# One stream of weights over two transformer blocks, the first block's layers written out, and the last modulation rows sent ahead of weights

## The reference

```
for l in range(2):
    h = x @ w_in[l]                      # all four branches and their gates
    ...                                  # RWKV-7, latent attention, convolution, attention over mem
    proj = einsum('bsnc,ncd->bsnd', branches, w_o_branch[l])
    gates = sigmoid(merge.reshape(B, S, 4, D) + b_gate[l])
    out = sum(gates * proj, axis=2) @ w_out[l]
    x = layer_norm(DEEPNORM_ALPHA * x + out, ln_g[l], ln_b[l])
```

```
for i in range(2):
    mod = silu(c) @ w_ada[i] + b_ada[i]              # and the same with c_ctx
    hx = rms_norm(x, g_mix[i]) * (1 + sc1) + sh1
    x = x + ga1 * (concat(attention, pool_mix, fourier_mix)(hx @ w_in[i]) @ w_out[i])
    x = x + ga2 * swiglu(rms_norm(x, g_ffn[i]) * (1 + sc2) + sh2)
```

## Time and profile before

| what | us |
|---|---|
| median of three runs | 3662.97 (3659.33 to 3665.39) |
| the profiled execution | 3664.74 |
| its span, first to last instruction | 3662.9 |
| PE busy | 3265.1 (89%) |
| PE weight loads | 2559.1 (70%) |
| DVE busy | 1445.6 (39%) |
| ACT busy | 1167.1 (32%) |
| POOL busy | 1485.3 (41%) |

### The profile page before, as it was taken

One profiled execution on the slowest core, in us unless ns is written; L12 is line 12 of the kernel. 1 busy time (PEld: TensorE's weight loads), 2 busy tenths in 40 slices (PEclk: granted clock), 3 DMA queues, 4 the chain that ended last, 5 costly groups with the idle time before them and its releaser, 6 DMA issues. The chain is left out here.

```text
span 3662.9 us, 53263 instructions
## 1 busy us (share of the span) xinstructions
PE 3265.1 (89%) x21306; PEld 2559.1 (70%) x21306; DVE 1445.6 (39%) x2330; ACT 1167.1 (32%) x1880; POOL 1485.3 (41%) x831
## 2 busy tenths in 40 slices
PE   6789999999677899999996888989999978889998
PEld 5674676788456746767874655778888865568786
DVE  4642265777645322757776225320000021530000
ACT  5213333322242234334222425332112232532121
POOL 4411553444243215534442236533334423745453
PEclk9999999999888999999998899999999989999999
DMA  3001122455120011225551200111111111022222
GB/s 110 16 11 50 63 88 75 167 195 198 39 86 8 20 46 58 94 67 183 191 190 35 97 35 1 47 58 64 58 64 64 64 55 46 1 75 98 87 98 81
DMA packets 75035, 282.21 MB, mean 77 GB/s; under 512 B 8320, under 2 KB 8320, under 8 KB 73888
## 3 DMA queue, kind: packets, MB, share of 16 engines
q1 hardware_dynamic: 74784, 278.76, 22.1%
HBM read 276.62 MB, written 2.10 MB: 76 GB/s over the span
## 5 line engine op out<-in xcount | busy, mean ns | idle before, releaser
L130 POOL TENSOR_TENSOR lows<-ring,highs 128x1024 fp32r<-128x1024 f32 x376 | 919.5, 2446 | 1734.1 <-ACT highs L122 1734.1
L154 PE MATMUL ps<-x_high,highs 128*128 128x512 f32 x1936 | 773.9, 400 | 81.2 <-ACT highs L122 67.7
L157 PE MATMUL ps<-x_low,highs 128*128 128x512 f32 x1936 | 760.6, 393 | 0.0
L122 ACT ACTIVATE highs<-ring 128x1024 fp32r<-128x1024 f32 x376 | 397.2, 1057 | 797.4 <-PE ps L154 458.5
L154 PEld LDWEIGHTS ps<-x_high,highs 128*128 128x128 f32 x1936 | 367.8, 190 | 170.9 <-ACT highs L122 70.0
L157 PEld LDWEIGHTS ps<-x_low,highs 128*128 128x128 f32 x1936 | 367.7, 190 | 78.3 <-issue 3.5
L585 PE MATMUL ps<-x_high,lows 128*128 128x512 f32 x1072 | 264.7, 389 | 0.0
L2350 DVE TENSOR_TENSOR hidden_scratch<-ps,hidden_scratch 128x512 f32<-128x512 f32 x66 | 39.7, 603 | 552.8 <-PE ps L1747 545.3
L585 PEld LDWEIGHTS ps<-x_high,lows 128*128 128x128 f32 x1072 | 201.2, 188 | 41.8
L162 PE MATMUL ps<-hidden_parts,highs 128*128 128x512 f32 (+1 forms) x528 | 189.9, 360 | 12.0 <-PEq L2284 12.0
L166 PE MATMUL ps<-hidden_parts,lows 128*128 128x512 f32 (+1 forms) x528 | 190.0, 360 | 0.0
(11 more groups left out here) (400 smaller groups left out, 5957.0 us busy)
## 6 DMA issues: line engine op xcount, KB each, us to landing
ring<-in_w SPq DMA_DIRECT2D x402, 512.0 KB, 3.5
merging<-in_ada SPq DMA_DIRECT2D x48, 512.0 KB, 4.3
BR<-in_ada SPq DMA_DIRECT2D x48, 512.0 KB, 4.3
more_tiles<-in_dft SPq DMA_DIRECT2D x2, 2048.0 KB, 8.3
X<-in_xT SPq DMA_DIRECT2D x4, 512.0 KB, 7.5
X<-in_memT SPq DMA_DIRECT2D x2, 1024.0 KB, 5.0
merging<-in_cond SPq DMA_DIRECT2D x4, 512.0 KB, 4.7
out<-xT SPq DMA_DIRECT2D x1, 2048.0 KB, 6.3
```

The lines of the kernel that those rows point to most:

```text
L122: nc.scalar.activation(self.high(n), self.chunk(n), ACT.Copy).then_inc(self.hi_made, 1)
L130: nc.gpsimd.tensor_tensor(self.low(n), self.chunk(n), self.high(n).bitcast(F32), ALU.subtract).then_inc(self.lo_made, 1)
L154: mm = nc.tensor.matmul(ps, high, xhigh, start=start, stop=False)
L157: nc.tensor.matmul(ps, high, xlow, start=False, stop=False)
```

## The change

The body of the first block's loop is written out for both layers (a Python loop), with tile names that carry the layer. One `Stream` now numbers all chunks of both blocks through; each stage adds the base of its layer, `send`, `hi` and `lo` stop at the end of all chunks, and the first chunk of a layer is counted in `used` like every other. The clearing stages behind the layers are gone, both in the first block and in the second. The out stage of the first block sends two chunks further and splits one more, as the down stages of the second block do at a layer's end. In most stages SP sends the one chunk that its slot allows before it clears, and the `cond` vectors and the `dft` table are also issued before the clears. At the end of the merge stage the rows 40 to 47 are all sent ahead of chunk 45.

```
--- before.py
+++ after.py
@@ class Stream
     def send(self, sp, upto):
-        for n in range(self.sent, upto):
+        for n in range(self.sent, min(upto, NCHUNKS)):
             last = n - RING
-            if last in self.splits:
-                sp.wait_ge(self.lo_made, self.splits.index(last) + 1)
+            if last in self.place:
+                sp.wait_ge(self.lo_made, self.place[last] + 1)
...
@@ build
+        def weights(n):
+            if n < SECOND:
+                return A["w1"][n // NCHUNK1, n % NCHUNK1, :, :]
+            return A["w2"][(n - SECOND) // NCHUNK2, (n - SECOND) % NCHUNK2, :, :]
+
+        split = [NCHUNK1 * layer + n for layer in range(LAYERS) for n in SPLIT1] + list(range(SECOND, NCHUNKS))
+        stream = Stream(WR, weights, split)
...
@@ attention
-            clear(sp, other)
             if beside is not None:
                 beside.send(sp)
+            clear(sp, other)
...
@@ first
-    with nc.Fori(0, LAYERS) as layer:
-        stream = Stream(WR, lambda n: A["w1"][bass.ds(layer, 1), n, :, :].rearrange("l p c -> p (l c)"), SPLIT1)
+    for layer in range(LAYERS):
+        base = layer * NCHUNK1
...
@@ first, merge
-                clear(sp, other)
                 for c in range(2):
                     sp.dma_start(CB[:, c, :], A["cond"][c].partition_broadcast(P)).then_inc(S("cond"), 16)
+                stream.send(sp, n0 + RING)
+                clear(sp, other)
                 for t in range(48):
-                    stream.send(sp, n0 + min(t + RING + (0 if t < 2 else 3), 48 + RING - 1))
+                    stream.send(sp, n0 + min(t + RING + (0 if t < 2 else 3), 45))
                     if t >= 4:
                         sp.wait_ge(S("ada"), 2 * (t - 3))
...
+                stream.send(sp, n0 + 48 + RING - 1)
@@ first, out
+                stream.send(sp, n0 + RING)
                 clear(sp, other)
-                stream.send(sp, n0 + 8)
+                stream.send(sp, n0 + 8 + RING - 1)
...
-                for t in range(3, 9):
+                for t in range(3, 10):
                     stream.hi(nc, act, n0 + t)
...
-                stream.lo(nc, pool, n0 + 8)
+                stream.lo(nc, pool, n0 + 9)
@@ behind each pass of the first block, and behind each layer of the second
-        S, other = stage()
-        with nc.Block() as block:
-            @block.sync
-            def _(sp):
-                clear(sp, other)
-                clear(sp, WR[3])
-                clear(sp, WR[4:])
@@ second, Norm.tensor
-                if n_first:
+                if n_first is not None:
                     nc.tensor.matmul(PS[:, 3, 0:1], C("ones", P), C("ones"), start=True, stop=True).then_inc(used, 1)
@@ second, mixing
+                sp.dma_start(Z[:, 0:8 * T], A["dft"]).then_inc(S("dft"), 16)
                 clear(sp, other)
-                sp.dma_start(Z[:, 0:8 * T], A["dft"]).then_inc(S("dft"), 16)
                 sp.wait_ge(S("dft"), 16)
@@ second, project (and the same in up)
+                    stream.send(sp, first + RING)
                     clear(sp, other)
-                    stream.send(sp, min(first + chunks + RING - 1, NCHUNK2))
+                    stream.send(sp, first + chunks + RING - 1)
```

More of the change, by code:

```diff
@@ L114, in hi @@
     def hi(self, nc, act, upto):
-        for n in range(self.hi_at, upto):
-            if n in self.splits:
-                s = self.splits.index(n)
+        for n in range(self.hi_at, min(upto, NCHUNKS)):
+            if n in self.place:
+                s = self.place[n]
                 self.wait(act, n)
@@ L198, in build @@
         XH, XL = sb("x_high", [P, DK, T], F32R)[:, :, :], sb("x_low", [P, DK, T], F32R)[:, :, :]
+        def weights(n):
[4 more added lines that the diff above has]
+        stream = Stream(WR, weights, split)
         with ExitStack() as one:
-            first(nc, one, A, PS, XH, XL, WR, mods, stage, loaded)
+            first(nc, one, A, PS, XH, XL, stream, mods, stage, loaded)
         with ExitStack() as two:
-            second(nc, two, A, PS, XH, XL, WR, mods, stage, constants, stored)
+            second(nc, two, A, PS, XH, XL, stream, mods, stage, constants, stored)
 def clear(sp, sems):
@@ L469, in _, with first @@
                     finish(pairs[i - 2].group)
-def first(nc, ctx, A, PS, XH, XL, WR, mods, stage, loaded):
+def first(nc, ctx, A, PS, XH, XL, stream, mods, stage, loaded):
     def sb(name, shape, dt=F32):
@@ L1425, in first @@
         room.close()
-        n0 = FIRST["merge"]
+        n0 = base + FIRST["merge"]
         room = ExitStack()
-        BL, BH = (room.enter_context(nc.sbuf_tensor(f"branches_{part}", [P, NB * WT, T], F32R))[:, :, :] for part in ("low", "high"))
-        Y = room.enter_context(nc.sbuf_tensor("merging", [P, 18 * T], F32))
+        BL, BH = (room.enter_context(nc.sbuf_tensor(f"branches_{part}{layer}", [P, NB * WT, T], F32R))[:, :, :] for part in ("low", "high"))
+        Y = room.enter_context(nc.sbuf_tensor(f"merging{layer}", [P, 18 * T], F32))
         def YT(i, n=1):
@@ L1539, in first @@
         room.close()
[L1540 removed]
+        n0 = base + FIRST["out"]
         room = ExitStack()
[L1542 to L1544 removed]
+        MH, ML = (room.enter_context(nc.sbuf_tensor(f"merged_{part}{layer}", [P, DK, T], F32R))[:, :, :] for part in ("high", "low"))
+        RR, SQ = (room.enter_context(nc.sbuf_tensor(name, [P, DK, T], F32))[:, :, :] for name in (f"residuals{layer}", f"residual_squares{layer}"))
+        Y = room.enter_context(nc.sbuf_tensor(f"merged{layer}", [P, 16 * T], F32))
         RST, RUN = YT(0), YT(1)
@@ L1679, with second @@
 NCHUNK2 = _at
-def second(nc, ctx, A, PS, XH, XL, WR, mods, stage, constants, stored):
+SECOND = LAYERS * NCHUNK1
+NCHUNKS = SECOND + LAYERS * NCHUNK2
+def second(nc, ctx, A, PS, XH, XL, stream, mods, stage, constants, stored):
     def sb(name, shape, dt=F32):
@@ L1712, in second @@
         update = layer < LAYERS - 1
-        stream = Stream(WR, lambda n: A["w2"][layer, n, :, :], list(range(NCHUNK2)))
-        used = WR[4]
+        base = SECOND + layer * NCHUNK2
+        used = stream.used
         room = ExitStack()
@@ L1732, in mark @@
         def mark(n, first):
-            return used if n and first else None
+            return used if first else None
         def gemm(pe, n, outs, ready=None):
```

61 lines of the change are left out of this document (28 added, 33 removed).

## The result

The changed kernel takes 3631.31 us (median of 4 runs, 3628.04 to 3635.67); the kernel before, in the same comparison, 3661.34 (3659.33 to 3665.39). The ratio is 0.9911, with a 95% interval of 0.9897 to 0.9924: 33 us less, give or take 5, by the ratio, 30.0 by the medians. Forecast were 3634 us and a range of 3615 to 3648. The profiled execution took 3628.04 us, the fastest of its four; its span is 3626.2 where the one before had 3662.9, its mean granted clock 0.960 where that had 0.956.

The account below looks back on a forecast made before the run. PE was taken to bound the stages, leaving its idle stretches to win: 37.9 us won less 6.8 lost, 31.1 net, from the profiled 3664.7 to 3634 us, with an 8-in-10 range of 3615 to 3648.

Parts of the forecast that it names:

- A: First block, layer 0 to 1: PE's 12.3 us wait shrinks to a 0.5 us stage change, gain 11.8 us.
- rival 4: Written-out code fetched late, or loop's end costs little: A gives perhaps half of its 11.8, 3640 us; chance 0.08.
- B: First block to second: earlier start (3.7) and one high part less in ACT's chain (0.9), gain 4.6 us.
- D: End of the program: output goes 0.5 us behind DVE in place of 3.7, gain 3.2 us.
- F: The `dft` table, twice: its transfer goes 3.2 us earlier, cutting PE's 7.91 us wait, gain 6.4 us.
- C: Second block, layer 0 to 1: 17.3 us up to PE's first product become 10.2, gain 7.1 us (3.2 to 8.5).
- E: Start of the merge stage, twice: third chunk goes some 3 us earlier, ACT can use 2.4, gain 4.8 us.
- G: End of the merge stage, twice: chunk 45, queued behind row 47, comes late and PE restarts later, cost 6.8 us.
- Rivals 1 and 3: Merge stage's end: 1, chunk 45 not late, 3612 us, chance 0.12; 3, G grows past the gains, 3679 us, chance 0.04.
- rival 1: Merge stage's end: chunk 45 is not late, so G wins 14.6 us instead of losing 6.8, 3612 us; chance 0.12.
- Rival 2: E and F are hidden and C gives only the removed stage, 3649 us; chance 0.13.
- H: Other sends ahead of clears, and clears behind the last send in the attention stage: both worth nothing.

Follow-up runs that it names:

- loop_out: Kernel before with only the first block's two layers written out in place of the loop: 3663.31 us, ratio 0.9995 to the kernel before.
- stages_back: Changed kernel with an empty stage of 50 clears put back at the end of each of the four layers: 3647.02 us, ratio 0.9937.
- cap50: Changed kernel with the merge stage's old transfer order, chunk 45 no longer queued behind row 47: 3630.44 us, ratio 0.9898.
- cap48: Changed kernel with rows 43 to 47 sent ahead of chunks 48 and 49 only, so not ahead of chunk 45: 3631.2 us, ratio 0.9901.
- clears_first: Changed kernel with the 50 clears put back ahead of each stage's first transfers, wherever they had been moved: 3644.78 us, ratio 0.9933.
- pace28: Like pace30, with the merge's 48 rows' sums spread over the first 28 products in place of 30: 3613.4 us, ratio 0.9848.
- pace30: Changed kernel with the merge queue's chunk lead over rows falling by one every 8 rows, no cap at chunk 45: 3611.92 us, ratio 0.9850.

## Why the prediction was right, point by point

A (layer 0 to 1 of the first block), forecast 11.8, is 11.94, and its step is shown in three parts. I had named the loop's jump as part of it without a price; it is a third. The rule that I cited from the Trainium skill, Runtime: NRT & Kernel Launch, Instruction fetch mechanics, that a taken branch out of the window stalls, fits the turn: 3 us without an instruction behind the taken branch, next to none where the same branch isn't taken. That those 3 us are fetching isn't shown by itself. Written-out code doesn't come late to an extent that shows: from PE's first matmul of a layer to its last pass 971.7 and 969.8 us, before 969.3 and 971.4, and loop_out isn't slower than the kernel before, so rival 4 is out.

B (first block to second), 4.6, is 4.60, with some luck: its start gave 3.96 and not 3.7, its chain 0.64 and not 0.9. D (the end), 3.2, is 3.4. F (the tables), 6.4, is 6.9.

C (layer 0 to 1 of the second block), 7.1, is 8.2, close to its upper bound of 8.5. The term that was mis-sized is the 5.6 us up to ACT's free moment: it measured 4.6, because PE's sums no longer ran at the low clock level behind the clearing stage. The sum took them over from the earlier trace rows as they were, and stages_back brings their 2.05 us back. The low part's 2.3 us stood as forecast. The bound of 8.5 had another reason, DVE's normalising not being held; it wasn't held, but PE waits for `x_low`, which ends behind POOL's low part all the same, so that bound held by luck.

E (start of the merge stage), 4.8, is 3.6, the term furthest off. Its step "the chunk goes some 3 us earlier" held: SP issues it 0.8 us behind PE's start of the stage in place of 3.9. But from issue to use it took 7.4 us (648.52 to 655.93) where it took 5.8 before (652.91 to 658.71), so ACT still waits 0.96. Ahead of it in the queue stand the two vectors, in both kernels, and moving the chunk ahead of them takes ACT's wait away. What made the transfer longer isn't shown.

G (end of the merge stage), 6.8 lost, is 6.3 by the milestones of the changed kernel, 9.6 against cap50 and 5.9 in the kernel before. Row 43's second sum ended at 903.9 and not at 906.0, and chunk 45 was used at 908.86 and not at 911.3, because the whole stage stood about 2 us earlier, while the sum for G is made in the times of the kernel before. PE's stall came out near the forecast (8.59 for 8.9), since PE was earlier by as much. Rivals 1 and 3 are out. What I had read wrongly in the earlier trace rows is the late rows' cause. I took the waits of 1.93 and 2.28 us for the whole of what the old order costs, and from this came rival 1's 7.3 us a layer for a queue that sends rows in time at the end. cap48 does that and gains nothing over cap50. The rows are late throughout the stage, behind chunks that wait for the ring, and at the end POOL's holds take the place of each wait that is removed.

Rival 2 (E and F hidden) is out by clears_first, and it bears out the first half of H: the other sends show nothing.

The forecast of 3634 us stood on the profiled execution of the kernel before, 3664.74; by the medians 30.0 us were gained and by the ratio 33, with 31.1 forecast. The agreement of the sum owes something to errors that cancel: C gave 1.1 more than forecast, E 1.2 less.

## What to carry to other kernels

A queue on which a send waits for one consumer and the next send for another makes the second consumer run at the first one's pace: here giving the rows more lead over their use was worth some 10 us of two merge stages, read against the old order at their end, and undoing the new order there about as much again. The new order at the end moved most of a stall from one place to another, and lost a few us by it. When a wait of an engine is taken away, look for what was hidden by it, in this kernel the 2.4 us instructions of POOL beside which DVE's take 2 us longer. And where a stage boundary is on the path, split it by one experiment each for the loop, the clears and the cold pipeline: here they were 4.0, 3.1 and 4.5 us, of which the loop alone, in the timing, would have passed for nothing. The clears are one instruction a semaphore, 50 of them in 2.8 us (649.0 to 651.8 in the changed kernel); clearing several at once, or none in some stages, wasn't tried.

## What the runs showed of the hardware that I had not expected

- Two-input instructions of DVE that begin beside a subtraction of POOL end behind it, by 1.1 us for a sum in both rows above, so the delay depends on the phase: 1.2 us sums took 2.0 when POOL's instruction had begun 1.5 us before, 3.4 when 0.1 before. Over a stage this averages out to a mean of 1.5 us a sum in the changed kernel and 1.9 to 2.0 in pace28, where DVE hardly pauses (15 us of 228).
- The end of a hardware loop's pass cost 4.0 us on the path, the exit 0.5, measured by writing the same two passes out; 3 us of the 4.0 pass between SP's taken branch and its next instruction.
- Fifty semaphore clears with their stage cost 3.1 us at two boundaries, 3.5 at the end and 4.5 where the parameters' transfer and ACT's normalising stand behind them. The last is 1.4 longer because PE's idle time ahead of its sums grows to 4.86 us and they run at the low clock level.
- The same four sums of PE, from layer 0 to 1 of the second block, ran at a granted clock of 0.87 behind 1.77 us of idle PE and at 0.50, the 1.2 GHz level, behind 4.86 and 5.20 us.
- The recurrence, the same in all kernels, ran with more stretches at the low clock level in one execution than in another: 3.1 us of difference between the traces of before and after in layer 1, 3.7 between those of pace30 and pace28 up to the merge stage of layer 0. That is as much as some of the terms above.
